# Selective attention: scores and softmax three units later, one selection round in each of eight units

## The reference

```python
q, k, v, qi, ki, wi = split(h @ w_in)                # 16 heads of 64; 8 index heads of 64
q, k = rope(rms_norm(q)), rope(rms_norm(k)); qi, ki = rope(qi), rope(ki)
idx   = einsum('bqhd,bsd->bqhs', qi_b, ki)
score = einsum('bqh,bqhs->bqs', wi_b, relu(idx))
score = where(visible, score, -inf)
top_val, top_idx = lax.top_k(score, n_sel)           # n_sel = 64 of 256 keys, for every query
logits = einsum(q_b, k[top_idx]) * HEAD_DIM ** -0.5
p = softmax(where(top_val > -inf, logits, -inf))
o = einsum(p, v[top_idx])
return o @ w_out
```

## Time and profile before

| | |
|---|---|
| median of 3 runs | 2417.49 us (2416.83 to 2418.04) |
| the profiled execution | 2416.02 us, its span 2414.2 us |
| PE busy | 2282.7 us (95%) |
| DVE busy | 1548.4 us (64%) |
| ACT busy | 1208.6 us (50%) |
| mean granted TensorE clock | 0.977 of full |
| selective attention | about 823 to 1019 |

### The profile page before, as it was taken

How to read it: one execution, slowest core, us unless ns; L and a number is a source line. 1 busy time by engine, 2 the same in 40 slices (tenths; PEclk the granted TensorE clock), 3 DMA queues, 4 the chain that set the end, 5 groups by cost and what they waited for, 6 DMA issues and landing times.

```text
span 2414.2 us, 55878 instructions
## 1 busy us (share of the span) xinstructions
PE 2282.7 (95%) x23148; PEld 2183.3 (90%) x23148; DVE 1548.4 (64%) x2372; ACT 1208.6 (50%) x2037; POOL 55.8 (2%) x83
## 2 busy tenths in 40 slices
PE   6899899999999989899988998999998999998998
PEld 5799799999999978799978997999897999887998
DVE  6854465566555688565588634655775777775776
ACT  5633454455544446454366334543675444675443
POOL 1000000000000010000010000000100000100000
PEclk8899999999999999999999999999999999999999
DMA  5310255533464433255433103555433554432553
GB/s 196 122 46 4 77 199 171 193 117 127 163 201 170 145 99 111 97 183 186 170 103 117 46 4 105 184 182 174 137 109 106 177 196 155 139 117 97 195 179 122
DMA packets 88437, 327.23 MB, mean 136 GB/s; under 512 B 9808, under 2 KB 9936, under 8 KB 87632
## 3 DMA queue, kind: packets, MB, share of 16 engines
q1 hardware_dynamic: 87984, 322.72, 39.6%
q0 software_dynamic: 288, 2.10, 0.3%
HBM read 323.73 MB, written 1.05 MB: 135 GB/s over the span
## 4 chain that ended last, share of the span: by engine, by line
PE 82%; DVE 9%; ACT 5%; issue 2%; DMA 0%; ACTq 0%; DVEq 0%
PE bank L1931 15%; PE bank L1932 15%; PE bank L1933 15%; PE bank L1953 5%; PE bank L1954 5%; PE bank L1955 5%; DVE w_split L2135 2%; PE bank L446 2%; ACT w_split L2026 2%; PE bank L455 1%; PE bank L1922 1%; PE bank L1353 1%; PE bank L1355 1%; PE bank L1354 1%; PE bank L469 1%
## 5 line engine op out<-in xcount | busy, mean ns | idle before, releaser
L1931 PE MATMUL bank<-h_split,w_split 128*128 128x256 f32 x3176 | 912.3, 287 | 18.1 <-DVE h_split L2157 8.0
L1933 PE MATMUL bank<-h_split,w_split 128*128 128x256 f32 x3176 | 897.3, 283 | 0.0
L1932 PE MATMUL bank<-h_split,w_split 128*128 128x256 f32 x3176 | 897.3, 283 | 0.0
L2135 DVE TENSOR_TENSOR w_split<-ring_a,w_split 128x1024 fp32r<-128x1024 f32 x474 | 568.3, 1224 | 218.4 <-ACT w_split L2026 217.3
L1931 PEld LDWEIGHTS bank<-h_split,w_split 128*128 128x128 f32 x3176 | 602.8, 190 | 29.7 <-DVE h_split L2157 11.3
L1932 PEld LDWEIGHTS bank<-h_split,w_split 128*128 128x128 f32 x3176 | 598.2, 188 | 1.5
L1933 PEld LDWEIGHTS bank<-h_split,w_split 128*128 128x128 f32 x3176 | 596.9, 188 | 0.0
L2026 ACT ACTIVATE w_split<-ring_a 128x1024 fp32r<-128x1024 f32 x474 | 483.4, 1050 | 39.0 <-PE bank L1933 33.6
L1953 PE MATMUL bank<-act_split,d_split 128*128 128x256 f32 x1008 | 285.7, 283 | 5.3 <-DVE act_split L2206 2.9
L1954 PE MATMUL bank<-act_split,d_split 128*128 128x256 f32 x1008 | 285.1, 283 | 0.0
L1955 PE MATMUL bank<-act_split,d_split 128*128 128x256 f32 x1008 | 285.0, 283 | 0.0
(11 more groups left out here) (272 smaller groups left out, 3298.3 us busy)
## 6 DMA issues: line engine op xcount, KB each, us to landing
ring_a<-wa SPq DMA_DIRECT2D x474, 512.0 KB, 3.9
ring_d<-wd SPq DMA_DIRECT2D x132, 512.0 KB, 4.1
tab_sb<-tab SPq DMA_DIRECT2D x1, 2448.0 KB, 13.6
hT<-na POOLq DMA_DIRECT2D x2, 1024.0 KB, 5.1
xT<-x SPq DMA_DIRECT2D x1, 1024.0 KB, 5.0
out<-xT SPq DMA_DIRECT2D x1, 1024.0 KB, 3.9
vec_sb<-vec SPq DMA_DIRECT2D x1, 288.0 KB, 5.0
tab_sb<-tab SPq DMA_DIRECT2D x1, 65.0 KB, 4.7
```

The lines of the kernel that those rows point to most:

```text
L1931: mm(dst, w[:, 0, ks], x[:, 0, k, :], start=(k == 0), stop=False)
L1932: mm(dst, w[:, 0, ks], x[:, 1, k, :], start=False, stop=False)
L1933: last = mm(dst, w[:, 1, ks], x[:, 0, k, :], start=False, stop=(k == KT - 1))
L2135: v.tensor_tensor(w_split[:, u % 4, 1, :], ring_a[:, u % 4, :], w_split[:, u % 4, 0, :].bitcast(f32), ALU.subtract).then_inc(s["w_lo"], 1)
```

## The change

`LAG` goes from 3 to 6: everything of pair t from `scores` to `out_low` lies three slots later (`scores(t)` in slot 18 + 3t, `shifted` in 19 + 3t, `pv` in 22 + 3t, `out_low` in 23 + 3t). `PV_AT` follows, so the bank rules stay the same. The eight selection rounds lie in slots 9 to 16, one in each, and the bias is made in slot 16 instead of 14. The output units lie in slots 30 + (0, 1, 2, 4, 6, 9, 12, 15). No instruction is added or removed.

```diff
-LAG = {"stick": 0, "dsa": 3, "multi": 0}
-PV_AT = {"stick": 8, "dsa": 13, "multi": 10}
+LAG = {"stick": 0, "dsa": 6, "multi": 0}
+PV_AT = {"stick": 8, "dsa": 16, "multi": 10}
-OUT_SLOTS = {"stick": (0, 1, 2, 3, 4, 5, 6, 7), "dsa": (0, 1, 2, 3, 4, 6, 9, 12), "multi": (0, 1, 2, 4, 5, 6, 8, 9)}
+OUT_SLOTS = {"stick": (0, 1, 2, 3, 4, 5, 6, 7), "dsa": (0, 1, 2, 4, 6, 9, 12, 15), "multi": (0, 1, 2, 4, 5, 6, 8, 9)}
...
                     if n == 9:
                         dve.wait_ge(s["idx_added"], IDX_HEADS)
-                    if 9 <= n <= 14:
+                    if 9 <= n <= 16:
                         take_eight()
-                    if n in (10, 13):
-                        take_eight()
-                    if n == 14:
+                    if n == 16:
                         step.did(v.tensor_scalar(index_scores, index_scores, TAKEN / 2, NEG, ALU.is_gt, ALU.mult))
                         step.settle()
```

## The result

The changed kernel takes 2423.66 us (median of 20 runs), the one before 2416.52 in the same series; the ratio is 1.0025, interval 1.0018 to 1.0032, so the change costs about 6 us (4.3 to 7.7) by that ratio; the medians differ by 7.1, inside the same interval. One run of the changed kernel took 5054.55 us and is left out of the ratio. The profiled execution of after takes 2424.63 us, its span is 2422.8, its granted clock 0.974.

What follows compares the result with a forecast made beforehand. PE was taken as the bound, held around the change by round trips through ACT and DVE. Tail +14.0 less front 3.9 gave +10.1 us, the median going from 2417.49 to 2427.6; range 2420.5 to 2431.0, its own 2426 to 2430.

Steps and rivals of the forecast that it cites:

- The sign and the mechanism: Whole kernel: slower by 10.1 us, the tail losing 14.0 through uncovered round trips and the front gaining 3.9; slower 0.81.
- The 0.5 us on DVE by slot 16: Selection: `evac`(16) comes 0.5 us earlier on DVE, at 907.1 instead of 907.61, with only `shifted(0)` gone from ahead of it.
- The front, 3.9 us: Selection and slots 18 to 21: unit 21 starts 3.9 us earlier, from 0.8 + 0.5 + 1.0 + 1.6; bounds 2.4 and 5.0.
- The tail at full clock, 52.6: First output unit to the layer's last unit's end: 52.6 us without low clock, against 45.5 before.
- The three idles: Tail: PE idles about 3 us ahead of each of units 4, 5 and 6, instead of one such idle before.
- the price of a fall of the clock: Tail: each of three idles costs 2.31 us of low clock, 6.9 in all; bounds 1.0 and 2.95 each.
- Rival 1: Tail: the clock falls only once or twice, not three times; +5.5 to +7.8 us, some 2424; chance 0.22.
- Rival 3: Selection: one round per slot frees PE from waiting for `norm_rope`; -7.1 us, 2410.4; chance 0.07.
- Rivals 4 and 5: Tail: 4, front gains nothing plus an extra wait, +13 to +15, 0.09; 5, idle time absorbs the extra pair, +0, 0.06.

Runs made afterwards that it cites:

- e1: Changed kernel with the eight selection rounds put back as before (slots 9 to 14, two in 10 and 13, bias in 14): 2423.90 us, ratio 1.0026 to before.
- e4: Kernel before with the rounds in slots 9 to 15, two only in slot 10, bias in slot 15: 2414.49 us, ratio 0.9992 to before.
- e10: Changed kernel with the rounds, one in each of slots 9 to 16, behind the `evac` of their slot: 2417.18 us, ratio 1.0002 to before.
- e2: Changed kernel with output units in slots 30 + (0, 1, 2, 5, 8, 11, 14, 15): 2403.38 us, ratio 0.9945 to before.
- e3: Kernel before with output units in slots 30 + (0, 1, 2, 3, 5, 8, 11, 12): 2405.94 us, ratio 0.9958 to before.
- e8: Changed kernel with `out_low` ahead of `lo` and of the second `normed` on DVE's queue: 2409.75 us, ratio 0.9971 to before.
- e5: Changed kernel with output unit 3 in the empty slot 33 instead of 34: 2424.55 us, ratio 1.0034 to before.
- e9: e3 with `out_low` ahead of `lo` and the second `normed`, and the selection rounds behind the `evac` of their slot: 2393.72 us, ratio 0.9912 to before.
- e12: e9 with the rounds in slots 9 to 15, two only in slot 10: 2395.51 us, ratio 0.9913 to before.

## Why the prediction came out as it did

- **The sign and the mechanism: right.** Slower, by the tail, with a front that gives back a third of it. Measured are +7.9 for the layer (profile), +7.1 between the medians and about +6 by the ratio, against +10.1.
- **The 0.5 us on DVE by slot 16: right** (0.54). e1 shows that it comes with the lag; the spread is worth nothing by itself (e1, e4).
- **The front, 3.9 us: right, 4.2 measured.** Unit 21 starts 50.43 us after `evac`(9) where it was 54.79, 4.4 earlier (forecast 3.9), and one of the three waits of "issue" is gone. The steady stretch is a copy, 0.1 us longer.
- **The tail at full clock, 52.6: right.** The starts of `pv`, units and scores, counted from the first output unit, were forecast step by step; the table has them.

| | forecast at full clock | after | after, less its low clock |
|---|---|---|---|
| unit 3 | 14.7 | 14.8 | 14.8 |
| `pv`(4) | 17.7 | 17.8 | 17.8 |
| unit 4 | 22.7 | 22.8 | 22.8 |
| scores of pair 6 | 26.2 | 27.7 | 26.2 |
| scores of pair 7 | 36.4 | 40.2 | 36.5 |
| end of the last unit (start + 2.95) | 52.6 | 57.6 | 52.6 |

The last column takes off what the units 4, 5 and 6 lost, 1.45, 2.30 and 1.28. The three idles stood where they were forecast, with 3.07, 2.95 and 2.94 us.
- **The step that failed: the price of a fall of the clock.** The prediction took 2.31 three times, 6.9. Measured are 1.45, 2.30 and 1.28, together 5.0. That is the largest part of the miss: 12.1 instead of 14.0 in the tail. The 2.31 is what unit 6 lost before: at a granted clock of 0.50, behind idles of 2.95 and 0.71 us, it takes 5.26 us instead of 2.95. The lower bound, 1.0, comes from the selection, where the clock fell behind 2.15 us of idle at 872.30. The upper bound, 2.95, was an estimate that no run shows: the unit at 1001.68 in after, whose 24 matmuls are all slow, loses 2.30. The one price known then was the highest of the four, and the sentence that the three idles are copies of it was true of the idles and not of the clock. The mean, 1.68, lies halfway between the prediction's value and its lower bound. 10.1, less 1.9 in the tail and 0.3 more in the front, leaves +7.9, the layer as measured.
- **From +7.9 in the layer to +7.1 between the medians or +6 by the ratio is not explained.** In this pair of profiled executions the unchanged mixers add +0.8, and the pair is 1.5 us further apart than the medians. The interval (4.3 to 7.7) nearly reaches the layer's figure, so no mechanism is needed, and none is shown.
- **The rivals.** Rival 1's figure (+5.5 to +7.8) is about what came out, but not by its mechanism: the clock fell three times, twice for a shorter time than priced. Rival 3, PE set free in the selection, did not happen; e10 shows what it would have needed. The argument against it, that DVE waits 2.10 us for ACT in the slot whatever the rounds do, held only for the order of the queue as it is: the round could not fill that wait because it stood behind it. Rivals 4 and 5 did not occur.
- **Where the loss could have been avoided.** e2, the changed kernel with the same number of units in other slots, is 0.55% faster than before. e3, with the old lag and rounds and filled slots, is 0.42% faster, so the gain is that of the slots. With filled slots the lag costs nothing that these runs show; the cost was the units' slots.

## What to carry to other kernels

When a dependent chain is moved later past the end of its covering work, write down for each step what independent unit stands between it and the next one. Where none does, keep some back: the same eight units, placed between `pv` and the next `turn` instead of where they became ready, made the tail 16 us shorter (9 with the shorter lag). And look at what a short instruction stands behind on its engine's queue: moving a 0.42 us instruction ahead of one that waits, and a round of selection behind the instruction whose result is awaited, change the order and no work. The first took 4.5 and 6.4 us out of the layers with filled slots (the 4.5 do not show in the times of the runs), the second 3.1 to 6.8. Spreading the rounds over more slots in the old order gave nothing.

## What the runs showed of the hardware that was not expected

**The same idle does not always bring the low clock, and the low clock does not always last as long.** Timeline of PE in the tail of e8, with the same code and the same idle twice:

```profile
990.69 0.66 PE L1309 MATMUL bank<-tab_sb,planes 128*128 128x128 f32 x4 [2.95 <-DVE planes L1722]
991.12 0.36 PE L1353 MATMUL bank<-o_split,w_split 128*128 128x256 f32 x1
...
999.69 1.11 PE L1309 MATMUL bank<-tab_sb,planes 128*128 128x128 f32 x4 [2.94 <-DVE planes L1722]
1000.46 0.56 PE L1353 MATMUL bank<-o_split,w_split 128*128 128x256 f32 x1
```

After 2.95 us at 990.69 everything runs at full rate (unit 994.07 - 991.12 = 2.95, clock 1.00 from 991 to 993); after 2.94 at 999.69 it does not (unit 1004.48 - 1000.46 = 4.02, clock 0.50 from 1001 to 1002.5). In the selection of after, three idles of 2.15 us differ too. The first, at 870.94, is followed by full clock (1.00 from 871 to 875); behind the second, at 886.08, the fall comes late (1.00 from 886 to 887.3, 0.50 from 887.8 to 890.5); behind the third, at 901.22, the two matmuls take 1.22 us instead of 0.70:

```profile
870.94 0.70 PE L1271 MATMUL bank<-dec,tab_sb 128*128 128x256 f32 x2 [2.15 <-ACT dec L1476]
```

```profile
886.08 0.70 PE L1271 MATMUL bank<-dec,tab_sb 128*128 128x256 f32 x2 [2.15 <-ACT dec L1476]
...
887.78 0.42 PE L1931 MATMUL bank<-h_split,w_split 128*128 128x256 f32 x1
...
901.22 1.22 PE L1271 MATMUL bank<-dec,tab_sb 128*128 128x256 f32 x2 [2.15 <-ACT dec L1476]
```

And an idle of 1.7 us, behind which the clock stayed full in before, was followed by a fall in e4. Its unit behind 1.70 us, with the code of before at 996.38, begins at full clock, falls within the unit (0.50 from 994 to 996), and takes 997.58 - 993.15 = 4.43 us:

```profile
993.15 0.36 PE L1353 MATMUL bank<-o_split,w_split 128*128 128x256 f32 x1 [1.70 <-DVE o_split L1729]
993.34 0.32 PE L1354 MATMUL bank<-o_split,w_split 128*128 128x256 f32 x1
993.47 0.41 PE L1355 MATMUL bank<-o_split,w_split 128*128 128x256 f32 x1
...
997.58 0.60 PE L1309 MATMUL bank<-tab_sb,planes 128*128 128x128 f32 x4
```

The unit at 996.38 took 2.95 behind 1.72. A price per idle thus ranges here from 0 to 2.3 us per unit of 24 matmuls. It is not scatter alone: e1, e5 and e10 have the tail of after with idles at nearly the same places, and their three slowed units lose 1.50, 2.31 and 1.32 us (e1), 1.34, 2.25 and 1.24 (e5), 1.32, 2.23 and 1.25 (e10), where after has 1.45, 2.30 and 1.28. So the price goes with the place in the tail; what sets it there was not tried.

**The mixers' length varies with no change of theirs**, as one profiled execution of each kernel shows. The second one took 299.5 us before, 301.6 in after and e1, 297.6 in e2, 297.1 in e9 and 301.8 in e12; the first between 295.5 and 299.8. The granted clock differs in them (0.74 and 0.83): the same stretch of the first mixer, in before and then in after.

```profile
110.00:130.00 20.00, 20.00 (x112) 17.77 (x112) 15.53 (x25) 7.25 (x13) 0.00 (x0) 0.74 0.38 125
```

```profile
110.00:130.00 20.00, 20.00 (x120) 17.55 (x120) 16.10 (x25) 8.49 (x16) 0.00 (x0) 0.83 0.41 132
```

So medians and layers can't agree to the microsecond: e2's median is 13.6 below before, its layer 8.2, and in its profiled execution the mixers give 4.9 of the difference. Whether such a kernel gets the shorter mixers in each run, and why, stays open.
